# Keys times state with row factors from memory, and the first stages of two tiles inside attention's last three steps

## The reference, cut to what matters

```python
def _gdn_mixer(q, k, v, z, b, a, conv_w, a_log, dt_bias, g_out, n_front):
    ...
    decay = jnp.cumsum(g, axis=-1)
    ...
    gamma = jnp.exp(jnp.where(tri, decay[..., :, None] - decay[..., None, :], -jnp.inf))
    kb = kc * beta[..., None]
    amat = jnp.eye(CHUNK, dtype=f32) + jnp.where(strict, jnp.einsum('bhncd,bhnsd->bhncs', kb, kc) * gamma, 0.0)
    u = lax.linalg.triangular_solve(amat, vc * beta[..., None], left_side=True, lower=True, unit_diagonal=True)
    w = lax.linalg.triangular_solve(amat, kb * jnp.exp(decay)[..., None], left_side=True, lower=True,
                                    unit_diagonal=True)
    aqk = jnp.where(tri, jnp.einsum('bhncd,bhnsd->bhncs', qc, kc) * gamma, 0.0)
    ...
    def step(S, xs):
        u_i, w_i, qd_i, kd_i, aqk_i, cd_i = xs
        v_new = u_i - jnp.einsum('bhcd,bhde->bhce', w_i, S)
        o = jnp.einsum('bhcd,bhde->bhce', qd_i, S) + jnp.einsum('bhcs,bhse->bhce', aqk_i, v_new)
        S = S * cd_i[..., None, None] + jnp.einsum('bhcd,bhce->bhde', kd_i, v_new)
        return S, o
    ...
def _hybrid_layer(...):
    ...
    y = jnp.concatenate([o_attn.astype(h.dtype), o_gdn], axis=-1) @ w_out
    return h + y
```

## Time and profile before

| | us |
|---|---|
| median of 3 runs | 910.07 (908.07 to 911.71) |
| the profiled execution | 908.99 |
| its span in the trace | 907.3 |
| PE busy (matmuls) | 842.7 |
| DVE busy | 611.9 |
| ACT busy | 387.9 |
| POOL busy | 247.4 |

### The profile page before, as it was taken

One profiled execution on the slowest core, in us unless ns is written; L12 is line 12 of the kernel. 1 busy time (PEld: TensorE's weight loads), 2 busy tenths in 40 slices (PEclk: granted clock), 3 DMA queues, 4 the chain that ended last, 5 costly groups with the idle time before them and its releaser, 6 DMA issues.

```text
span 907.3 us, 16786 instructions
## 1 busy us (share of the span) xinstructions
PE 842.7 (93%) x6500; PEld 511.1 (56%) x6500; DVE 611.9 (67%) x1400; ACT 387.9 (43%) x1228; POOL 247.4 (27%) x254
## 2 busy tenths in 40 slices
PE   6999899999899999999799999977899899899897
PEld 2554344444456666666366666655766556556554
DVE  2443899999999999996475666647455456455432
ACT  3434677667954555554455554522122022022010
POOL 8000100000003645666447321013322222223200
PEclk9999999999999999999699999987699999999999
DMA  6242200130030020001010000061002101112011
GB/s 176 74 179 93 70 24 23 36 127 23 25 116 0 1 92 1 1 0 47 23 48 25 25 25 24 14 235 57 3 1 71 38 35 71 36 37 71 26 47 47
DMA packets 26624, 46.98 MB, mean 52 GB/s; under 512 B 3304, under 2 KB 10768, under 8 KB 26544
## 3 DMA queue, kind: packets, MB, share of 16 engines
q1 hardware_dynamic: 26000, 45.79, 14.7%
...
## 4 chain that ended last, share of the span: by engine, by line
PE 82%; DVE 8%; ACT 4%; issue 3%; DMA 1%; SPq 1%; POOL 0%; DVEq 0%; ACTq 0%
PE ps L1557 19%; PE ps L1788 12%; PE ps L1535 11%; PE ps L1412 5%; PE ps L1608 5%; PE ps L1597 4%; PE ps L1579 4%; PE ps L1691 2%; PE ps L1509 2%; PE ps L1727 2%; DVE areaQ L1262 1%; PE ps L1752 1%; PE ps L1744 1%; PE ps L1463 1%; PE ps L1683 1%
## 5 line engine op out<-in xcount | busy, mean ns | idle before, releaser
L1093 DVE TENSOR_SCALAR_CACHE_REDUCE junk<-scores,iw 128x272 bf16<-128x272 f32 (+6 forms) x224 | 213.6, 954 | 8.2
L1557 PE MATMUL ps<-areaH,areaW 128*128 128x384 f32 (+1 forms) x576 | 168.1, 455 | 1.6 <-ACT areaQ L832 1.6
L1557 PEld LDWEIGHTS ps<-areaH,areaW 128*128 128x128 f32 x576 | 109.4, 190 | 59.9 <-issue 1.8
L1788 PE MATMUL ps<-areaW,areaQ 128*128 128x512 f32 x256 | 123.1, 613 | 8.9 <-DVE areaQ L1378 8.9
L648 POOL TENSOR_TENSOR staging<-staging,areaC 128x520 f32<-128x520 f32 x60 | 88.2, 1509 | 63.3 <-ACT areaC L870 63.3
L1788 PEld LDWEIGHTS ps<-areaW,areaQ 128*128 128x128 f32 x256 | 44.9, 191 | 48.9 <-issue 37.8
L936 ACT COPY scores<-ps 128x128 f32<-128x128 f32 x35 | 9.3, 266 | 146.2 <-PE ps L1711 146.2
L665 POOL TENSOR_TENSOR areaW<-scores,tmp 128x256 f32<-128x256 f32 (+1 forms) x64 | 43.5, 704 | 79.4 <-DVE small L1179 69.3
L1412 PE MATMUL ps<-areaW,areaH 128*128 128x460 f32 (+1 forms) x144 | 59.6, 569 | 2.1 <-DVE areaH L1015 2.0
L684 POOL TENSOR_TENSOR areaH<-areaH,masks 128x512 f32<-128x512 f32 x26 | 30.1, 1159 | 106.2 <-PE ps L1711 51.2
L870 ACT ACTIVATE areaC<-areaC,small 128x520 f32<-128x520 f32 x60 | 42.5, 723 | 32.8 <-POOL staging L648 32.8
...
## 6 DMA issues: line engine op xcount, KB each, us to landing
...
```

The lines of the kernel that those rows point to most:

```text
L1093: tlink(V.tensor_scalar(junk[:, 0:n], scores[:, SC0[i]:SC0[i] + n], at, init, op, ALU.add, accum_out=cnt[:, i - 1:i]))
L1557: ins = mm(ps[:, n % 4, 0:hi - lo], wslot[:, g % 2, k, 128 * m:128 * m + 128], hT[:, k, lo:hi], start=k == 0, stop=k == KD - 1)
L1788: ins = mm(ps[:, 6 + half_, :], y, wslot[:, half_, k, :], start=k == 0, stop=k == 7)
```

## The change

Six things are changed together.

1. **Row factors.** The stage `rb` has no PE part any more. rv1 and rv2 are turned once, in attention's step 22 (`turn_rows`, one transpose, one DVE copy), stored to memory (`row_factor_scratch`, 72 rows of 128), and for each tile two DMAs of 256 KB each spread them over the 128 partitions of `rowb` in SBUF (`load_rows`), double-buffered by tile. The DVE additions and the exponential for the queries read `rowb` in the place of PSUM.
2. **Keys times state.** The stage `w`, its ACT copy and kbe are gone. A stage `ks` multiplies the keys with the state of the tile before (4 matmuls), DVE subtracts that, scaled, from bv (`corrected`, 4 instructions), and `v` is the inverse times the corrected bv alone.
3. **Pace.** New tiles begin every 8 slots (PACE) instead of 9, the stages of `REC_AT` follow the tile's own last pre stage at once, p4 and p5 share a slot, and `yt` and `ks` share one.
4. **Run-out.** Ten entries of tiles 0 and 1 (`RUN_OUT`) stand inside attention's steps 32, 33 and 34 on all four engines. PE's wait for `s_on` = 8 moves to tile 0's `v`.
5. **Buffers** are dealt out again, so that what the run-out writes isn't read by attention any more.
6. POOL's two waits at the start of the recurrence are gone, and SP loads rows ahead of each tile's other loads.

The core of the diff (the stages' bodies moved into a function `recurrent(entries)` on each engine, otherwise unchanged, are left out):

```diff
...
+FIRST = [0, 0] + [len(pre_list(0)) + PACE * k for k in range(NT - 2)]
+RECUR = [FIRST[t] + len(pre_list(t)) for t in range(NT)]
+REC_AT = [(["v"], []), ([], ["os"]), (["p0"], []), (["p1"], ["g"]), (["p2"], ["yt", "ks"]), (["p3"], ["c"]),
+          (["p4", "p5"], []), (["p6", "p7", "fin"], [])]
...
+        older = [t for t in range(NT) if t == 0 or slot - FIRST[t] >= PACE]
+        for t in older:
+            pre(t)
         rec(0)
-        for t in range(1, NT):
-            if first_slot(t) > slot - HALF:
-                order += pre(t)
+        for t in range(NT):
+            if t not in older:
+                pre(t)
         rec(1)
-    return order
+        order.extend((t, "rb") for t in range(2, NT) if FIRST[t] == slot + 1)
...
+RUN_OUT = [([(0, "rb")], [(0, "nat"), (1, "rb")]), ([(0, "kk")], [(1, "nat"), (0, "cc")]),
+           ([(1, "kk")], [(0, "x2"), (1, "cc")])]
+def run_out_first(slots):
+    first = [entry for step in RUN_OUT for part in step for entry in part]
+    return first, [entry for slot in slots for entry in slot if entry not in first]
...
+        rowb = areaH[:, 6 * T:6 * T + 2048].rearrange("p (s c h t) -> p s c h t", s=2, c=2, h=HG)
...
+                if st == SQP + len(SQ) + 3:
+                    now.append(("rows", 0, "D"))
...
+            def load_rows(t):
+                if t >= 2:
+                    sp.wait_ge(g_dve, DV(t - 2, "gq"))
+                    if t > 2:
+                        sp.wait_ge(g_act, AC(t - 2, "eq"))
+                src = rv_d.rearrange("(c t h) n -> t c (h n)", c=2, h=4)[t]
+                for c in range(2):
+                    sp.dma_start(rowb[:, t % 2, c].rearrange("p h t -> p (h t)"),
+                                 src[c].partition_broadcast(128)).then_inc(s_rvl[t % 2], 16)
...
+                if i == NB - 1:
+                    sp.wait_ge(*ring_read(AT_RING["rows", 0]))
+                    sp.dma_start(rv_d, sums[0:2 * NT * 4, 0:128]).then_inc(s_rvd, 16)
+                    sp.wait_ge(s_rvd, 16)
+                    load_rows(0)
+                    load_rows(1)
...
+                if t + 1 < NT:
+                    load_rows(t + 1)
...
-            pool.wait_ge(s_on, NB)
-            pool.wait_ge(s_oo, 16 * NB)
...
-                        A(qd[r_], heads(2 * s_ + 1), ACT.Exp).then_inc(g_act, 1)
+                            A(qd[r_], rowb[:, s_, 1], ACT.Exp).then_inc(g_act, 1)
...
+                if step >= NP:
+                    for entries in RUN_OUT[step - NP]:
+                        recurrent(entries)
...
-                V.tensor_tensor(kbe[s_][0:n], bank(2 * s_)[0:n], per_head(skbe[0:n, t], n), ALU.mult).then_inc(g_dve, 1)
...
-                dve.wait_ge(g_pe, PE(t, "rb"))
+                dve.wait_ge(s_rvl[s_], 32 * (t // 2 + 1))
                 if t >= 2:
                     dve.wait_ge(g_pool, PO(t - 2, f"m{levels(t - 2)[-1]}"))
-                V.tensor_tensor(AT[s_][0:n, :, 0:n], bank(2 * s_)[0:n, :, 0:n], all_heads(maskS[0:n, 0:n], n, n),
+                if t >= 4:
+                    dve.wait_ge(g_pe, PE(t - 4, "s"))
+                V.tensor_tensor(AT[s_][0:n, :, 0:n], rowb[0:n, s_, 0, :, 0:n], all_heads(maskS[0:n, 0:n], n, n),
                                 ALU.add).then_inc(g_dve, 1)
-                V.tensor_tensor(aq[r_][0:n, :, 0:n], bank(2 * s_ + 1)[0:n, :, 0:n], all_heads(maskI[0:n, 0:n], n, n),
+                V.tensor_tensor(aq[r_][0:n, :, 0:n], rowb[0:n, s_, 1, :, 0:n], all_heads(maskI[0:n, 0:n], n, n),
                                 ALU.add).then_inc(g_dve, 1)
+            def corrected(t):
+                r_ = t % 4
+                dve.wait_ge(g_pe, PE(t, "ks"))
+                for h in range(HG):
+                    V.scalar_tensor_tensor(bv[r_][:, h, :], bank(4)[:, h, :], skbe[:, t, h:h + 1], bv[r_][:, h, :],
+                                           ALU.mult, ALU.add).then_inc(g_dve, 1)
...
+                if step == NP:
+                    dve.wait_ge(s_red, 2 * NP)
+                    dve.wait_ge(s_ring, AT_RING["turn", G0[NP - 2] - 1] + 1)
+                    glink(V.memset(AT[0], 0.0))
+                    assert g[0] == G_ALL, g
+                if step >= NP:
+                    recurrent(RUN_OUT[step - NP][0])
+                for what, k, who in RING[step]:
+                    if who == "D" and what != "meta":
+                        read_ring(what, k)
+                if step >= NP:
+                    recurrent(RUN_OUT[step - NP][1])
...
+            def turn_rows():
+                pe.wait_ge(s_gd, G_CB)
+                b = fill("rows", 0)
+                turn(ps[0:2 * NT * 4, b, 0:128], rv, ident).then_inc(s_ring, 1)
...
+                    elif stage == "kk":
+                        pe.wait_ge(g_dve, DV(t, "bv"))
...
+                    elif stage == "ks":
+                        pe.wait_ge(g_dve, DV(t - 1, "s"))
+                        for h in range(HG):
+                            ins = mm(col(4, h), conv4[:, 1, h, cols], S[:, h, :], start=True, stop=True)
+                        ins.then_inc(g_pe, 1)
+                    elif stage == "v":
+                        pe.wait_ge(g_dve, DV(t, f"ttf{levels(t)[-1]}"))
+                        pe.wait_ge(g_dve, DV(t, "u" if t else "bv"))
+                        if t == 0:
+                            pe.wait_ge(s_on, NB)
+                        for h in range(HG):
+                            ins = mm(ps[0:n, 4, 128 * h:128 * h + 128], TTf[r_][0:n, h, 0:n], bv[r_][0:n, h, :],
+                                     start=True, stop=True)
+                        ins.then_inc(g_pe, 1)
+                    elif stage == "os":
+                        pe.wait_ge(g_dve, DV(t, "vnew"))
...
+                if step >= NP:
+                    if step == NP:
+                        pe.wait_ge(s_red, 2 * NP)
+                    recurrent(RUN_OUT[step - NP][0])
...
-                elif stage == "rb":
-                    for b, rv, name in ((b0, rv1, "kdec"), (b1, rv2, "bv")):
-                        pe.wait_ge(g_dve, DV(t, name))
-                        for h in range(HG):
-                            ins = turn(col(b, h, n), rv[0:n, t, h:h + 1].broadcast_to([n, 128]), ident[0:n, 0:n])
-                    ins.then_inc(g_pe, 1)
...
-                elif stage == "w":
-                    pe.wait_ge(g_dve, DV(t, f"ttf{levels(t)[-1]}"))
-                    for h in range(HG):
-                        ins = mm(col(b0, h, n), kbe[s_][0:n, h, :], TTf[r_][0:n, h, 0:n], start=True, stop=True)
-                    ins.then_inc(g_pe, 1)
-                elif stage == "v":
-                    pe.wait_ge(g_act, AC(t, "w"))
-                    if t:
-                        pe.wait_ge(g_dve, DV(t - 1, "s"))
-                    for h in range(HG):
-                        o = ps[0:n, 4, 128 * h:128 * h + 128]
-                        ins = mm(o, TTf[r_][0:n, h, 0:n], bv[r_][0:n, h, :], start=True, stop=t == 0)
-                        if t:
-                            ins = mm(o, wT[r_][:, h, :], S[:, h, :], start=False, stop=True)
-                    ins.then_inc(g_pe, 1)
...
```

483 lines of the change are left out of this document (243 added, 240 removed).

## The result

881.56 us (median of 4 runs, 881.48 to 885.48) against 909.07 for the kernel before on the same chip: a ratio of 0.9705, 95% interval 0.9668 to 0.9742. 876 was forecast, 865 to 890. Of all runs here a single execution, one of four in the run on order (1388.94 us, granted clock 0.556), was in the chip's slow state, and it is left out of that run's median.

What follows compares the result with a forecast made beforehand. PE's own work was taken to bound the steady part, latency and the clock the start. 584.12 plus the stretches and a 4.36 tail gave a span of 873.8; with 1.69 and 1.08 added, 876 us, range 865 to 890.

Steps and rivals of the forecast that it cites:

- A: From the start of attention's step 32 to tile 1's x2: 20.5 us in place of 33.52.
- B: From tile 1's x2 to its output: 31 us in place of 40.76, ends 26 and 36.
- C: From tile 1's output to the end of its p7: 28 us, ends 26.3 and 30.
- D to G: Stretches between ends of p7, tiles 1 to 8: 33.2, 128.45 (four periods of 31.7), 25.4 and 18.8 us.
- rival 2: Freed time turns into waits at x8, y8, x32, yt: A 26, periods 33.0 instead of 31.7, 888 us; chance 0.15.
- E: Four steady periods, ends of p7 of tiles 2 to 6: 128.45 us, one clock dip of 1.6 us kept.
- those of the periods: Steady part: ends of p7 stand 31.7 us apart, PE busy for about 29, wait for yT still the largest.
- those of the start: Tile 1's x2 within 2 us of 604.6, output about 635.6; L1288 waits once, 1 to 3 us, at tile 2.
- The first: Rival: the clock stays high through the recurrence's start, B 26 and C 26.5, total 869.5 us; chance 0.17.
- The third: Rival: steady periods lose the high clock, slower than before, 924 us with 8 us at half clock in each of six; chance 0.03.
- The fourth: Rival: A and B don't shrink, bound by tiles 0 and 1's inverse through DVE; 895 us; chance 0.05.

Runs made afterwards that it cites:

- run on order: Changed kernel with ks of the next tile ahead of yt and DVE's yT copy ahead of the younger tile's merge: 870.29 us (ratio 0.9572).
- quiet run: Changed kernel with five of sixteen weight slices and tile 2's rows loaded during attention, all other loads behind tile 1's x8: 877.27 us (ratio 0.9638).
- rhythm run: Changed kernel with five of sixteen weight slices loaded early in attention, the others two at a time behind tiles 1 and 2's loads: 881.0 us (ratio 0.9715).

## Why the prediction was right, and where it was not

**A** (20.5, measured 21.08) was right in its sum and in the new wait: PE's fourth group stood 1.08 us for the copy behind ACT's exponentials, where 0.9 was worked out. cc and x2 of tile 1 waited 0.99 and 1.19.

```profile
596.98 0.84 PE L1661 MATMUL ps<-small,areaH 128*128 128x128 f32 x6 [1.08 <-ACT areaW L440]
```

Its story gave the gain to the ten entries put into the steps. The run without them puts 2.2 us there; the other 10.2 of the 12.4 us stay wherever the entries stand, and most of them go with the rows from memory. So the sum of A was right for a reason that is largely another, which is luck. (Its terms add up to 604.4 and not to 604.6.)

**B** (31, measured 39.21) is the step that failed. "By subtraction, at this stretch's own prices" took over a stretch whose transfers had ended (a DMA share of 0.01 in the earlier trace rows) for one that begins 10 us earlier, right in the 4 MB load. The load was thought of only as what delays the rows of tile 2, plus 1.5 us for DVE. No such wait showed: PE had been stopped first, and DVE came late itself. In its place PE's own instructions came late, as the packets on q8 show. Both pauses together are 6.49 us against the 0.81 of before, 5.7 of the 8.2 missing us. The quiet run gives back 4.60 of them. The other 2.5 us are in the size of the rest: 32.72 without pauses, and up to 33.9 where the clock rises later, against a forecast of 30.2 without its old pause. Of that, 1.15 us were gone in the rhythm run with its earlier clock (31.57). The half clock stood for 30.7 of B's 39.21 us, and for 27 of the 40.76 of before, while the forecast kept the old prices; how much of the rest this makes was not taken apart.

**C** (28, measured 26.23) was marked up by 1.7 for a low clock that had ended 3.5 us before it. **D to G** hold within 0.5 us each. The period is 32.15 instead of 31.7: the wait for yT stayed (1.48), y8 waits 0.61, and a wait of 0.73 before yt, of which rival 2 had spoken, came instead of the ones at x8 and x32:

```profile
740.70 0.46 PE L1767 MATMUL ps<-tmp,areaH 128*32 128x32 f32 x32 [0.61 <-DVE areaH L1270]
755.51 0.66 PE L1811 MATMUL ps<-small,areaQ 128*128 128x128 f32 x4 [0.73 <-DVE areaQ L1368]
```

The dip of 1.6 us that E kept from before did not come, and that hid the 0.45 per period.

**The total** came closer than its terms. In the profiled execution the span is 9.9 us above the forecast of 873.8: 2.2 at the start, 0.6 in A, 8.2 in B, less 1.8 in C, and 0.6 behind. The median execution is 3.9 us shorter than the profiled one, where 1.1 longer had been added (875.5 and 1.08 make 876.6, not 876), and that brings the miss down to 5.6. That C's error and the choice of execution helped is luck. Of the signs, those of the periods held (32.15 apart, PE busy for 29.2); those of the start did not (x2 at 607.4, the output at 646.6, and no wait of L1288 for a row load).

The first row addition lost 0.38 us against the second, beside a POOL product that began at 740.20 and ran 0.51 us into it. That is the sign which the Trainium skill, SBUF — State Buffer, section "Who interferes with whom", gives for two such instructions, at half the 0.74 allowed for it. The 0.74 came from a product that ran 0.88 us into the spread, so the loss goes with the overlap. Nothing waits for it.

```profile
740.20 1.38 POOL L726 TENSOR_TENSOR scores<-scores,masks 128x512 f32<-128x512 f32 x1 [4.08 <-PE ps L1751]
...
741.07 1.06 DVE L1288 TENSOR_TENSOR scores<-areaH,small 128x512 f32<-128x512 f32 x1
742.05 0.68 DVE L1290 TENSOR_TENSOR areaQ<-areaH,small 128x512 f32<-128x512 f32 x1
```

**The rivals.** The first (clock high, B 26) was tested: even at 0.94 the stretch is 30.4, since DVE's and ACT's queues are next in line. The second came in two of its four spots only, for 0.45 us in a period, and A is 21.08 and not 26. The third did not happen, but the run with 9 slots shows that it was a near neighbour: one slot without projection work loses all of the gain. The fourth was right that B would hardly shrink (40.76 to 39.21), but not in its reason: without the long pauses and with ACT's queue cleared it is 30.3.
